# The loop over four expert pairs, written out with every body once per pair

## What is computed

```python
def moe_swiglu(h, w_router, b_router, w_gate_up, w_down):
    tok = h.reshape(bsz * seq, d)
    logits = (tok @ w_router).astype(jnp.float32) + b_router.astype(jnp.float32)
    probs = jax.nn.softmax(logits, axis=-1)
    top_p, top_i = lax.top_k(probs, TOP_K)                    # 2 of 8
    top_p = top_p / jnp.sum(top_p, axis=-1, keepdims=True)
    gates = jnp.sum(jax.nn.one_hot(top_i, N_EXPERTS, dtype=jnp.float32) * top_p[..., None], axis=1)
    out = jnp.zeros_like(tok)
    for e in range(N_EXPERTS):                                # swiglu: silu(h @ gate) * (h @ up) @ down
        out = out + gates[:, e:e + 1].astype(tok.dtype) * swiglu(tok, w_gate_up[e], w_down[e])
    return out
```

## Time and profile before

| | us |
|---|---|
| median of three runs | 1569.91 (1568.47 to 1571.96) |
| the profiled execution | 1568.5 |
| its span in the trace | 1566.7 |
| TensorE busy in the span | 1391.6 (89%) |
| VectorE busy | 664.2 (42%) |
| ScalarE busy | 499.8 (32%) |
| change from pair 0 to 1, 1 to 2, 2 to 3 | near 845, 1082 and 1317 |

### The profile page before, as it was taken

The page is one execution under the profiler, slowest core; times in us unless marked ns, Lnnn a source line. Parts: engine busy times, 40 slices in busy tenths (PEclk is TensorE's granted clock), DMA queues, the critical chain, the costliest instruction groups (busy, mean ns, idle before and its releaser), DMA issues.

```text
span 1566.7 us, 25857 instructions
## 1 busy us (share of the span) xinstructions
PE 1391.6 (89%) x11115; PEld 986.4 (63%) x11116; DVE 664.2 (42%) x769; ACT 499.8 (32%) x561; POOL 35.2 (2%) x66
## 2 busy tenths in 40 slices
PE   4999999999998798999997999997788887797786
PEld 2763788888684646777674777674575664463433
DVE  5933444454301725755452755552664551100003
ACT  2323534343201513444442444443353541000001
POOL 2001000000100001000000000000000000000000
PEclk8989999999999897999999999999798999799899
DMA  8785875454754024499999689999789999899993
GB/s 298 283 323 204 314 289 212 164 205 170 292 191 161 1 98 175 159 360 410 411 412 409 258 331 410 412 411 409 286 324 411 413 413 407 316 412 412 413 412 128
DMA packets 206823, 474.63 MB, mean 303 GB/s; under 512 B 9986, under 2 KB 10030, under 8 KB 206670
## 3 DMA queue, kind: packets, MB, share of 16 engines
q1 hardware_dynamic: 199968, 470.83, 77.8%
q10 hardware_dynamic: 6702, 1.71, 0.5%
HBM read 471.47 MB, written 1.05 MB: 302 GB/s over the span
## 4 chain that ended last, share of the span: by engine, by line
PE 70%; DMA 11%; SPq 7%; issue 6%; DVE 4%; ACT 2%; ACTq 1%; DVEq 0%; POOL 0%
PE ps L2233 34%; PE ps L2504 9%; SPq L489 7%; DMA ring<-in_moe_w_down_dram 7%; PE ps L2516 6%; PE ps L2316 4%; DMA ring<-in_ada_w_dram 2%; PE ps L2380 2%; PE ps L2044 2%; PE ps L2209 2%; PE ps L2324 2%; PE ps L2449 1%; DMA ring<-in_moe_w_gate_up_dram 1%; PE ps L2459 1%; DVE arena L1222 1%
## 5 line engine op out<-in xcount | busy, mean ns | idle before, releaser
L1797 DVE TENSOR_TENSOR ring_lo<-ring,w 128x2048 fp32r<-128x2048 f32 x126 | 288.4, 2290 | 175.9 <-ACT w L991 143.2
L991 ACT ACTIVATE w<-ring 128x2048 fp32r<-128x2048 f32 x126 | 240.6, 1912 | 233.7 <-PE ps L2233 232.0
L2504 PE MATMUL ps<-ring,arena 128*32 128x128 f32 (+1 forms) x5376 | 254.7, 301 | 53.6 <-DMA ring<-in_moe_w_gate_up_dram 27.3
L2504 PEld LDWEIGHTS ps<-ring,arena 128*32 128x32 f32 (+1 forms) x5376 | 192.2, 119 | 116.5 <-issue 61.5
L2233 PE MATMUL ps<-ring_lo,x_hi 128*128 128x512 f32 x560 | 220.2, 393 | 0.0
L2233 PE MATMUL ps<-w,x_hi 128*128 128x512 f32 x336 | 137.1, 408 | 15.8 <-DVE ring_lo L1797 13.7
L2233 PE MATMUL ps<-w,x_lo 128*128 128x512 f32 x336 | 132.5, 394 | 0.0
L1457 DVE TENSOR_TENSOR ring_lo<-ring,w_hi 128x2048 fp32r<-128x2048 f32 x42 | 95.6, 2290 | 85.8 <-ACT w_hi L767 85.8
L2233 PEld LDWEIGHTS ps<-ring_lo,x_hi 128*128 128x128 f32 x560 | 106.3, 190 | 20.1
L2516 PE MATMUL ps<-ring,tri 128*32 128x512 f32 (+1 forms) x448 | 75.3, 690 | 28.3 <-DMA ring<-in_moe_w_down_dram 26.4
L767 ACT ACTIVATE w_hi<-ring 128x2048 fp32r<-128x2048 f32 x42 | 78.8, 1909 | 50.0 <-PE ps L2233 42.0
(11 more groups left out here) (391 smaller groups left out, 1578.8 us busy)
## 6 DMA issues: line engine op xcount, KB each, us to landing
ring<-in_moe_w_gate_up_dram SPq DMA_DIRECT2D x112, 2048.0 KB, 16.7
ring<-in_moe_w_down_dram SPq DMA_DIRECT2D x56, 2048.0 KB, 18.2
ring<-in_ada_w_dram SPq DMA_DIRECT2D x24, 2048.0 KB, 11.1
ring<-in_ffn_w_gate_up_dram SPq DMA_DIRECT2D x14, 2048.0 KB, 11.8
ring<-in_ffn_w_down_dram SPq DMA_DIRECT2D x7, 2048.0 KB, 7.6
ring<-in_sb_w_qkv_dram SPq DMA_DIRECT2D x6, 2048.0 KB, 8.6
ring<-in_s_w_out_dram SPq DMA_DIRECT2D x2, 2048.0 KB, 7.7
ring<-in_sb_w_out_dram SPq DMA_DIRECT2D x2, 2048.0 KB, 14.2
```

The source lines that it names most:

```text
L991: act.activation(half3(h).bitcast(F32R), ff_half(gran(pair_place(*main_granule(n))), half), ACT.Copy).then_inc(whi_done, 1)
L1797: dve.tensor_tensor(ff_half(ring_lo[place % RING][:, :], half).bitcast(F32R), ff_half(gran(place), half), half3(h), ALU.subtract).then_inc ...
L2504: ins = pe.matmul(dst[width * r:width * r + width, 0:cols], x[:, k, 0:width], weights[:, k, cols * r:cols * r + cols], start=k == 0, stop= ...
```

## The change

The loop over pairs goes. Every engine's program holds four pairs one behind the other, each with its own four tests and five bodies. `BODY_ORDER` says which body stands first, right behind the tests of a pair; the four others follow, and each body ends with an unconditional jump to the tests of the next pair, without a prefetch hint. The kinds of all pairs are read once, ahead of the first. In the last pair the jump goes out of the routed part.

As the pair's number is now a constant, waits compare with constants. `tails` and `split` are gone: a body that skips the tail or the split counts their semaphores up by what it skips, on instructions of `next_gather` and `next_out`. The split of x for the next pair moves from the start of the body into `pair_end` of the pair before (`x_round`, `x_rest`), ahead of the jump. `scatter_pair` moves into each body. In the last pair the gather for a fifth pair is left out, and `gate_diag`, `gate_row` and `gate_copy` of gate 3 stand inside its body, in the banks 0 and 1.

```diff
+BODY_ORDER = ((0, 1, 2, 3, 4), (0, 1, 2, 3, 4), (1, 0, 2, 3, 4), (2, 1, 0, 4, 3))
...
-        def expert_pairs(eng, p):
...
+        def pair_kinds(eng):
+
+            return [eng.value_load(cnt_i[0:1, 4, p:p + 1], min_val=0, max_val=4) for p in range(PAIRS)]
+
+        def pair_by_kind(eng, name, p, kind, wide, light):
+
+            bodies = (lambda: wide(True, TAIL), lambda: wide(False, TAIL), light, lambda: wide(True, W2),
+                      lambda: wide(False, W2))
+            order = BODY_ORDER[p]
+            label = lambda k: f"{name}_pair{p}_kind{k}"
+            test = lambda i: f"{name}_pair{p}_test{i}"
+            end = f"{name}_pair{p}_end"
+            entry, came_from = nc.cur_bb, {}
+            for i, k in enumerate(order[1:], 1):
+                came_from[k] = came_from[order[0]] = nc.cur_bb
+                after = test(i + 1) if i + 1 < len(order) else label(order[0])
+                eng.br_eq(kind, k, on_true=label(k), on_false=after)
+                if i + 1 < len(order):
+                    nc.switch_bb(after)
+            for k in order:
+                with nc.body(label(k), parent=came_from[k], valid_engines=[eng.engine]):
+                    bodies[k]()
+                    eng.br(end)
+            nc.switch_bb(end, parent=entry)
...
-                pair_weights(0, AHEAD)
-                with sp.Fori(1, PAIRS) as p:
-                    pair_weights(p, 0)
+                for p in range(PAIRS):
+                    pair_weights(p, 0 if p else AHEAD)
...
+            def x_round(p):
+
+                act.wait_ge(xe_act, 2 * p + 2)
+                act.wait_ge(xe_dve, p + 1)
+                for half in range(2):
+                    act.activation(x3_hi[:, 4 * half:4 * half + 4, :].bitcast(F32R), xe[:, 4 * half:4 * half + 4, :],
+                                   ACT.Copy).then_inc(xhi_done, 1)
...
                 pair_out(p, light)
                 silu_second(p, FB - 1, width)
-                next_out(p + 1)
+                if p + 1 < PAIRS:
+                    next_out(p + 1, skipped)
                 turned_second(p, FB - 1, width)
+                if p + 1 < PAIRS:
+                    x_round(p + 1)
                 second_results(p)
...
-                next_out(p + 1)
+                if p + 1 < PAIRS:
+                    next_out(p + 1, skipped)
+                else:
+                    gate_diag(3)
                 product_second(p, FB - 1, width)
+                if p + 1 < PAIRS:
+                    x_rest(p + 1, 0)
+                else:
+                    gate_copy(3)
                 wait_used2(dve, p, "bd", FB - 1)
                 dve.tensor_copy(ysb4[0:64, 3, :], ps[0:64, Y_BANK + 3, :]).then_inc(ysb_dve, 1)
+                if p + 1 < PAIRS:
+                    x_rest(p + 1, 1)
...
-                with nc.Fori(0, PAIRS, engines=[dve.engine], hint_back_edge=True) as p:
-                    tails, split, by_kind = expert_pairs(dve, p)
-                    by_kind(lambda tail, width: pair_wide(p, tails, split, tail, width), lambda: pair_light(p))
+                kinds_now = pair_kinds(dve)
+                for p in range(PAIRS):
+                    pair_by_kind(dve, "dve", p, kinds_now[p], lambda tail, width: pair_wide(p, tail, width), lambda: pair_light(p))
...
                 second_in(p, "bg", FB - 1, width)
-                next_gather(p + 1)
+                if p + 1 < PAIRS:
+                    next_gather(p + 1, skipped)
                 second_in(p, "bu", FB - 1, width)
                 second_down(p, FB - 2, width)
+                if p + 1 == PAIRS:
+                    pe.wait_ge(m_aT, PAIRS * FB)
+                    gate_row(3)
                 second_turn(p, FB - 1, width)
                 second_down(p, FB - 1, width)
                 scatter_first(p)
+                scatter_pair(p)
```

More of the change, by code:

```diff
@@ L977, in turned_second, with pair_wide @@
                 act.activation(dst, src, ACT.Copy).then_inc(n_aT, 1)
-            def pair_wide(p, tails, split, tail, width):
+            def pair_wide(p, tail, width):
                 def w_round(h):
@@ L1041, in pair_wide @@
                         w_round(2 * n + 8)
-                pair_end(p, width, False)
+                pair_end(p, width, False, 0 if tail else 1)
             def pair_light(p):
@@ L1770, in product_second, with x_rest, pair_end @@
                                   ALU.mult).then_inc(n_act, 1)
-            def pair_end(p, width, light):
-                next_selection(p)
-                second_selection(p + 1)
+            def x_rest(p, half):
+                k = slice(4 * half, 4 * half + 4)
+                dve.wait_ge(xhi_done, 2 * p + 2 + half + 1)
+                dve.tensor_tensor(x3_lo[:, k, :].bitcast(F32R), xe[:, k, :], x3_hi[:, k, :], ALU.subtract
+                                  ).then_inc(xlo_done, 1)
+            def pair_end(p, width, light, skipped):
+                if p + 1 < PAIRS:
+                    next_selection(p)
+                    second_selection(p + 1)
                 if not light:
@@ L1806, in product_tail @@
                     if tail:
[L1807 to L1808 removed]
+                        dve.wait_ge(t_silu, p * FB + f + 1)
+                        dve.wait_ge(t_up, p * FB + f + 1)
                         dve.tensor_tensor(sgt, sgt, ps[:, S_BANK, TAIL_UP:TAIL_UP + P], ALU.mult).then_inc(t_act, 1)
[L1811 to L1815 removed]
                 w_rest(0)
@@ L1863, in pair_light @@
                         product_second(p, f - 1, W2)
-                pair_end(p, W2, True)
+                pair_end(p, W2, True, 2)
             with dve.If(paired(dve) > 0):
                 dve.memset(rt[:, 0, 72:73], 0.0).then_inc(sc_done, 4 * PAIRS)
+                for half in range(2):
+                    x_rest(0, half)
                 second_selection(0)
-                with nc.Fori(0, PAIRS, engines=[dve.engine], hint_back_edge=True) as p:
-                    tails, split, by_kind = expert_pairs(dve, p)
-                    by_kind(lambda tail, width: pair_wide(p, tails, split, tail, width), lambda: pair_light(p))
+                kinds_now = pair_kinds(dve)
+                for p in range(PAIRS):
+                    pair_by_kind(dve, "dve", p, kinds_now[p], lambda tail, width: pair_wide(p, tail, width), lambda: pair_light(p))
             with dve.Else():
@@ L2673, in pair_wide @@
                         second_turn(p, f - 1, width)
-                pair_end(p, width)
+                pair_end(p, width, 0 if tail else 1)
             def pair_light(p):
@@ L2722, in pair_light @@
                         second_turn(p, f - 1, W2)
-                pair_end(p, W2)
+                pair_end(p, W2, 2)
             with pe.If(paired(pe) > 0):
                 pe.transpose(ps[:, T_BANK, 0:P], ident[:, :], ident[:, :]).then_inc(sc_ps, 4 * PAIRS)
-                with nc.Fori(0, PAIRS, engines=[pe.engine], hint_back_edge=True) as p:
-                    tails, split, by_kind = expert_pairs(pe, p)
-                    by_kind(lambda tail, width: pair_wide(p, tails, split, tail, width), lambda: pair_light(p))
-                    scatter_pair(p)
+                kinds_now = pair_kinds(pe)
+                for p in range(PAIRS):
+                    pair_by_kind(pe, "pe", p, kinds_now[p], lambda tail, width: pair_wide(p, tail, width), lambda: pair_light(p))
             with pe.Else():
```

125 lines of the change are left out of this document (62 added, 63 removed).

## The result

| | before | after |
|---|---|---|
| median of the runs | 1569.19 us (4 runs, 1568.47 to 1571.96) | 1533.56 us (4 runs, 1532.65 to 1537.05) |
| profiled execution: its time, span | 1568.5, 1566.7 us | 1537.05, 1535.3 us |

The ratio is 0.977, with a 95% interval of 0.975 to 0.979: 35.6 us less. The forecast was 1537.5 us. The profiled execution of the changed kernel is the slowest of its four, 3.5 us above their median, so the two traces differ by 31.4 us only.

A forecast was written before the change was run, and what follows sets the result against it. Weight transfers were taken to bound the expert stage, with queue idle time to win: 6.0 + 12.1 + 9.0 + 6.1 - 1.0 = 32.2 us off 1568.5 gives 1536.3, plus 1.4 for the median, forecast 1537.5 us; range 1530 to 1552.

The forecast's parts named there:

- 0 to 1: Change from pair 0 to pair 1: TensorE's work 4.6 us earlier, full clock 1.4 us more; 6.0 us gained.
- 1 to 2: Change from pair 1 to pair 2: one late instruction arrival instead of three; 12.1 us gained, 9 to 13.5.
- 2 to 3: Change from pair 2 to pair 3: one late arrival instead of four, gain limited by transfers to 9.0 us.
- the end: Behind the last weights: fifth pair's gather dropped, gate work moved earlier, one VectorE jump; 6.1 us gained, 3 to 7.
- the entry: Ahead of the first pair: four loads and four tests for three loads and one test; 1.0 us lost.
- What bounds: Expert stage: weight transfers bound it at 412 GB/s, and only time with the transfer queue standing still can be won.
- Rival (a): A second late block of instructions behind each far jump: gain only 20 us, 1549.5 us; chance 0.17.
- Rival (c): Another kind runs than the body placed first, a second far jump of some 5.6 us per change: 1549 us; chance 0.03.
- (b): Transfers are not the bound at 2 to 3, or the clock stays full everywhere: 1528 to 1532 us; chance 0.08.
- (d): Slower: TensorE's longer code pauses 1.25 us at many blocks; with 40 pauses 1586 us; chance 0.07.

The follow-up runs named there:

- before_nohint: The kernel before the change, without the prefetch hint for the pair loop's branch back on ScalarE, VectorE and TensorE: 1576.77 us.
- wrong_last: Changed kernel with only pair 3's bodies in order of kinds, a second far jump per engine at 2 to 3: 1538.53 us; repeated, 1535.09 us.
- wrong_second: Changed kernel with only pair 1's bodies in the order 1, 0, 2, 3, 4, a second far jump at 0 to 1: 1542.2 us.
- wrong_third: Changed kernel with only pair 2's bodies in the order 0, 1, 2, 3, 4, a second far jump at 1 to 2: 1540.03 us.

## Why the prediction was right, and where not

Each gain in the terms of the sum, beside the idle queue that went:

| term | predicted | distance from the copy | idle queue |
|---|---|---|---|
| 0 to 1 | 6.0 | 5.1 | 5.8 |
| 1 to 2 | 12.1 | 13.1 | 13.6 |
| 2 to 3 | 9.0 | 11.4 | 9.4 |
| the end | 6.1 | 7.4 (from the last wait for weights) | |
| the entry | -1.0 | -0.1 | |

The distances are those from the copy to the up product, and at 2 to 3 to the second product of the light body.

- **What bounds.** Right: up to the last wait for weights the gain is idle time of the transfer queue. The kernels range from 23 us of idle sum at 1534 us to 52 at 1569 and 57 at 1577.
- **0 to 1.** The jump of 5.9 us and the full clock came as written, and the first work stood 7.45 us behind the copy, where the working had 8.1 (844.09 to 852.2). The first work came 5.3 us earlier against the copy (4.6 in the working) and the clock gave 1.4 us (1.4 in the working), 6.7 in all. Missing in the working was what is late next, the down granule: of the 6.7 us 5.1 were left at the up product. The 1.4 us are partly luck. The working scales 34 matmuls in 1.42 us to 64 in 1.9, but they scale to 2.7, which leaves 0.6 us; and it leaves out that the 30 matmuls behind them ran at half clock too (1.93 us) and that a pause of 2.13 us would come where 1.25 had been. From the start of the first product to the end of the second it is 8.3 us before and 6.9 after.
- **1 to 2.** The order was right: ScalarE's new far jump (5.26 us from copy to rounding), its rounding, then VectorE. VectorE started 7.2 us behind the copy where the sum had 8.0 (from 1102.1 to 1089.8 is 12.3 us, where the working has 12.1). ScalarE paid 4.66 us here, as the working had it with "now has a far jump as well". The reading of the earlier trace rows was right too, and `before_nohint` gives its cause, which I had not seen: the loop's hint served ScalarE.
- **2 to 3.** Right in size and for the reason given. TensorE came 11.4 us earlier, not 17: the jump took 7.4 us and a block was late by 3.9. The 9 us of idle queue set the gain, so this cost nothing. The kernel without jumps shows it best: its second product comes 9 us earlier still, and the last pair is no shorter. In `wrong_last` and `wrong_last_again` one more jump left the weight stretch as it was. In the two traces pair 3 takes 8.6 us less to the last wait for weights.
- **The end.** 1.3 us too small by this trace, and 0.3 us too large by the second one of the changed kernel (48.1 us where this one has 46.6). In this one the down product started 26.9 us behind the last wait for weights, not 27.5, and GpSimd's part was done before VectorE came to need it, so that the 0.6 us put down to it were not paid.
- **The entry.** 0.9 us too pessimistic. Four loads and tests cost as much as three loads and one test had.
- **Rival (a)**, the second late block, came in what the traces show of it (pauses of 2.13 us at 0 to 1 and 3.90 us at 2 to 3, one jump of 7.4 us) and was wrong as a price: both places are covered, the first by a wait for a granule, the second by a full queue. The Trainium skill (Runtime: NRT & Kernel Launch, "Instruction fetch mechanics") calls the cost of crossing into the next block mostly hidden. No row says that the two pauses are such crossings. If they are, the cost was not hidden from the engine, only from the kernel's time.
- **Rival (c)**, put at 1549, did not come, and its price was near: it charged 5.6 us each at 0 to 1 and 1 to 2 and nothing at 2 to 3. Taken one at a time, the times rose by 8.6 us (`wrong_second`) and 4.3 us (`wrong_third`), 12.9 for the 11.2, and the weight stretch by 6.3 and 1.5 us; at 2 to 3 it did not grow. No run had a second jump at all three changes. What the price missed is the half clock and VectorE's sums at 0 to 1.
- **Rivals (b) and (d)** did not come: the queue moved 411 GB/s in the window of the last pair, and from 640 us to the end TensorE's idle time without a releaser ahead of the products of L2549 adds to 7.4 us, in four pieces.

By the traces the terms add to 26.4 + 7.4 - 0.1 = 33.7 us, where the forecast had 32.2. Against them stand 2.2 us lost ahead of the change in the profiled execution, which took 1537.05 us where 1536.3 were forecast for it. The median lies 3.9 us below its forecast because that execution is 3.5 us above the median. The idle queue adds to 28.8 us where the stretch from the first expert matmul to the last wait for weights gives 26.4; the 2.4 us between them are not placed.

**What is left** is 16.5 and 6.8 us of idle queue in pairs 1 and 2. Most of it is no longer jumps, since it stays in the kernel without any (16.9 and 6.3 us). In 870 to 920 us TensorE is busy 49.45 of 50 us while the queue moves 276 GB/s. The queue stands still because the seven places are full: SyncE's loads wait in this window for TensorE to be done with a place (us in total, times, the longest):

```profile
SPq L487 <- PE ps L2268: 45.4, 4, 18.5
```

Just before, TensorE had waited for the first down granule. None of the kernels tried has a lower median than the changed one.

## What to carry to other kernels

Count the far jumps that each engine takes one behind the other, and price them with branch rows of the same trace (on TensorE 5.2 to 7.4 us here beside transfers, 3.3 to 3.8 us without). Then ask of each which other limit it lies beside: after the loop was written out, taking away the remaining jumps gave nothing that the times show and 3 us at most by the traces, and adding one cost 6 to 9 us at the first change, some 2 to 4 at the second and nothing up to the last weights at the third, though the three look alike in the code. TensorE's sequencer jumped while the engine worked off the scatter, so that at 0 to 1 the work placed ahead of the jump covered all but 0.5 us of it. In a stage that lives on transfers, the queue's idle time over a few windows is a better measure of an edit than the waits of any engine, and the distance between two fixed events of the trace (879.9 and 880.0 us in two executions of one kernel) agrees between executions of one kernel better than the times do.

## What the runs showed of the hardware that was not expected

- A prefetch hint for a plain jump out of a long body cut TensorE's jump from 5.9 and 6.0 us to 0.34 and 0.42 us, but left one of four at 5.84 us; set nearer to the jump, it left that one at 1.86 us, and ScalarE still idled 4.85 and 5.53 us behind its own jumps.
- A jump of 5.9 us cost TensorE 0.5 us of its own time: the sequencer took it while the engine worked off 7 us of queued scatter.
- The hint of a loop's branch back, with another far jump between it and the branch, still took 1.8 us off TensorE's branch (7.0 to 5.2 us) and made ScalarE's free at one of three changes (2.47 against 17.22 us of idle time): 7.5 us of the kernel's time.
- A fall through the tests is no guarantee against late instructions: TensorE paused for 3.90 us after seven matmuls of a body that it had run into, in two profiled executions, and for 3.14 us at the same place in `wrong_third`. There was no pause when the body was reached by a jump, nor without jumps or with hints.
- Behind a wait of 5.75 to 5.9 us for weights, the same 32 matmuls of one kernel took 5.05 us in one execution and 6.63 us in another; the granted clock there was 0.72 and 0.53.
